# A streaming encoder layer on one core: the input projection by seven products for eight, with token normalisation and rotary tables moved to the first stage

## The reference

```python
h = rmsnorm(x, g_mix)
proj = h @ w_in + b_in                       # 1024 x 2304
qa = rotary(proj[..., :512]);  ka = rotary(proj[..., 512:640]);  va = proj[..., 640:768]
qb, kb, vb = proj[..., 768:1280], proj[..., 1280:1792], proj[..., 1792:]
oa = window_sink_gqa(qa, ka, va, sinks)      # 8 query heads, 2 key heads, window of 128
ob = chunk_relbias_attention(qb, kb, vb, rel_bias)   # 8 heads, own and 8 chunks before
x = x + concat(rmsnorm(oa), rmsnorm(ob)) @ w_out
x = x + memory_cross_attention(rmsnorm(x), rmsnorm(mem), ...)
h = rmsnorm(x, g_ffn)
x = x + (silu(h @ w_gate) * (h @ w_up)) @ w_down
return rmsnorm(x, g_final)

def rotary(t, positions):                    # heads of 64, halves of 32
    ang = positions[..., None] * inv_freq
    t1, t2 = t[..., :32], t[..., 32:]
    return concat([t1 * cos(ang) - t2 * sin(ang), t2 * cos(ang) + t1 * sin(ang)])
```

## Time and profile before

| | us |
|---|---|
| median of 3 runs | 2964.43 (2963.25 to 2970.74) |
| the profiled execution | 2965.04 |
| its span, first to last instruction | 2963.2 |
| PE busy | 2784.1 (94%) |
| DVE busy | 1598.7 (54%) |
| POOL busy | 1052.1 (36%) |
| ACT busy | 1063.8 (36%) |

### The profile page before, as it was taken

The page is one execution under the profiler, slowest core; times in us unless marked ns, Lnnn a source line. Parts: engine busy times, 40 slices in busy tenths (PEclk is TensorE's granted clock), DMA queues, the critical chain, the costliest instruction groups (busy, mean ns, idle before and its releaser), DMA issues. The chain is left out here.

```text
span 2963.2 us, 39417 instructions
## 1 busy us (share of the span) xinstructions
PE 2784.1 (94%) x14112; PEld 2353.4 (79%) x14112; DVE 1598.7 (54%) x2913; ACT 1063.8 (36%) x2101; POOL 1052.1 (36%) x756
## 2 busy tenths in 40 slices
PE   7898989979999899799998799999999998999998
PEld 7786868769999788688887588888788887788876
DVE  3247446457779533233333566666766665654354
ACT  5333333246666422233332333333333332222242
POOL 6644344311100011311222555555555553453152
PEclk9899999979999999899999899999999999999999
DMA  7655666476575433312223433335433333744454
GB/s 237 221 186 197 225 217 215 151 178 158 142 165 136 150 128 128 127 61 75 86 75 114 163 105 97 97 105 170 143 107 96 104 107 113 274 141 145 147 169 131
DMA packets 244535, 428.47 MB, mean 145 GB/s; under 512 B 17792, under 2 KB 151424, under 8 KB 239104
## 3 DMA queue, kind: packets, MB, share of 16 engines
q1 hardware_dynamic: 222416, 406.15, 43.0%
q10 hardware_dynamic: 21936, 19.93, 2.4%
HBM read 285.50 MB, written 135.27 MB: 142 GB/s over the span
## 5 line engine op out<-in xcount | busy, mean ns | idle before, releaser
L50 PE MATMUL gu_acc<-gu_t,shared_m 128*128 128x512 f32 x880 | 344.4, 391 | 10.0 <-DVE gu_t L2348 6.5
L51 PE MATMUL gu_acc<-gu_t,shared_m 128*128 128x512 f32 x880 | 343.9, 391 | 0.0
L52 PE MATMUL gu_acc<-gu_t,shared_m 128*128 128x512 f32 x880 | 343.7, 391 | 0.0
L334 POOL TENSOR_TENSOR front_wq_lo<-front_wq_raw,front_wq_hi 128x1024 fp32r<-128x1024 f32 x72 | 179.1, 2489 | 234.0 <-ACT front_wq_hi L330 233.4
L1424 PE MATMUL att_sum_o<-att_v,att_turned_sb 128*128 128x64 f32 x1616 | 203.0, 270 | 0.0
L50 PEld LDWEIGHTS gu_acc<-gu_t,shared_m 128*128 128x128 f32 x880 | 166.1, 189 | 46.2 <-issue 6.9
L1424 PEld LDWEIGHTS att_sum_o<-att_v,att_turned_sb 128*128 128x128 f32 x1616 | 197.2, 193 | 0.2
L52 PEld LDWEIGHTS gu_acc<-gu_t,shared_m 128*128 128x128 f32 x880 | 166.2, 189 | 34.6
L51 PEld LDWEIGHTS gu_acc<-gu_t,shared_m 128*128 128x128 f32 x880 | 166.1, 189 | 34.6
L1394 PE MATMUL att_sum_s<-att_k,att_q 128*128 128x320 f32 (+3 forms) x704 | 146.1, 327 | 25.4 <-DMA att_k<-qk_d 25.1
L330 ACT ACTIVATE front_wq_hi<-front_wq_raw 128x1024 fp32r<-128x1024 f32 x72 | 76.3, 1059 | 251.1 <-PE qkv_acc L52 149.1
(11 more groups left out here) (310 smaller groups left out, 7310.8 us busy)
## 6 DMA issues: line engine op xcount, KB each, us to landing
front_wq_raw<-in_w_in SPq DMA_DIRECT2D x72, 512.0 KB, 5.2
down_a<-a_d SPq DMA_DIRECT2D x37, 704.0 KB, 4.1
ahead_w_even<-in_w_gate SPq DMA_DIRECT2D x44, 512.0 KB, 4.4
more_w_odd<-in_w_up SPq DMA_DIRECT2D x44, 512.0 KB, 4.3
a_d<-gu_a_mix SPq DMA_DIRECT2D x88, 256.0 KB, 3.1
att_k<-qk_d SPq DMA_DIRECT2D x36, 512.0 KB, 13.2
a_d<-gu_a SPq DMA_DIRECT2D x66, 256.0 KB, 4.2
shared_m<-a_d SPq DMA_DIRECT2D x19, 704.0 KB, 4.3
```

The lines of the kernel that those rows point to most:

```text
L50: pe.matmul(out, l_hi, r_hi, start=first, stop=False)
L51: pe.matmul(out, l_hi, r_lo, start=False, stop=False)
L52: return pe.matmul(out, l_lo, r_hi, start=False, stop=last)
L334: pool.tensor_tensor(self.lo[:, i % Q_SLOTS, :], self.raw[:, i % Q_SLOTS, :], raw(self.hi[:, i % Q_SLOTS, :]), ALU.subtract).then_inc(self ...
```

## The change

The projection is done in two halves of 1024 tokens. In a half, features are taken as 9 pairs of tiles, and tokens as two blocks of 512; with the contraction cut in two this is a 2 x 2 by 2 x 2 product of blocks, done in 7 products of 12 matmuls (4 over half the contraction, three each). POOL makes the combined weights, DVE the four results from the seven products. The order of the pairs is `PAIRS_IN`: `u` is kept as it is, `v` values, `r` rotated queries, and `x` holds rotated keys and the other values.

The token operands of the seven products are made in `stage_products`, which normalises and transposes all 16 token tiles; ACT copies each transposed tile whole (`whole`), DVE makes four combinations of each pair of tiles (`mix_pair`), and SP stores all seven operands to `t_d`. `stage_qkv` loads them, ACT rounds and DVE subtracts. The operand of product 0 and the first weights are loaded at the end of `stage_products` (`ahead`, a class that gate-and-up uses too, with two operands). The sines and cosines of all tokens are also made in `stage_products`, stored to `trig_d` and loaded by half.

The rotated tiles hold first halves of four heads in one tile and second halves in the other, row by row, so that no swap is needed: POOL multiplies by the sine, DVE by the cosine and adds. Attention reads them back with a stride over the rows (`qk_d` has 14 tiles instead of 13). The table of relative positions is made for one head at a time instead of four.

```diff
-        SQUARE, SCALE, TURN = (2, 6, 24, 40), (3, 7, 28, 41), (5, 14, 34, 43)
-        RSQRT, LOAD = (6, 10, 15, 19), (5, 5, 11, 15)
+        TURN = [stage_at(j, 0) for j in range(NT)]
+        SCALE = [stage_at(j, -3) for j in range(NT)]
+        SQUARE = [stage_at(j, -7) for j in range(NT)]
+        WHOLE = [stage_at(j, 2) for j in range(NT)]
+        MIX = [stage_at(2 * i + 1, 5) for i in range(HT)]
+        PUT = [stage_at(j, 6) for j in range(NT)]
+        PUT_MIX = [stage_at(2 * i + 1, 12) for i in range(HT)]
+        TABLE = [[at_share((16 + 22 * b + 5 * part) / 106) for part in range(4)] for b in range(N_BLK)]
...
+                sp.wait_ge(s_plain[0], 16 * 3 * UNITS // 2)
+                sp.wait_ge(s_plain[1], 16 * 3 * UNITS // 2)
+                sp.wait_ge(s_mst, 16 * 4 * UNITS)
+                ahead.load(sp)
+                store(GROUPS - 1)
...
+                def mix_pair(i):
+                    dve.wait_ge(rows.s_lo, 2 * MT + 4 * i + 4)
+                    if i >= 1:
+                        dve.wait_ge(s_mst, 64 * i)
+                    first, second = h[:, 2 * i % 4, :, :], h[:, (2 * i + 1) % 4, :, :]
+                    h11, h21, h12, h22 = first[:, 0:KH, :], first[:, KH:KT, :], second[:, 0:KH, :], second[:, KH:KT, :]
+                    t1, t2, t3, t4 = (mixed[:, m, :, :] for m in range(4))
+                    dve.tensor_tensor(t1, h12, h11, ALU.subtract).then_inc(s_mixed, 1)
+                    dve.wait_ge(s_mixed, 4 * i + 1)
+                    dve.tensor_tensor(t2, h22, t1, ALU.subtract).then_inc(s_mixed, 1)
+                    dve.tensor_tensor(t3, h22, h12, ALU.subtract).then_inc(s_mixed, 1)
+                    dve.wait_ge(s_mixed, 4 * i + 2)
+                    dve.tensor_tensor(t4, t2, h21, ALU.subtract).then_inc(s_mixed, 1)
...
+        PAIRS = len(PAIRS_IN)
+        KP = HALVES * PAIRS
+        TOTAL = KP * N_PROD
+        RESULT = {1: 0, 4: 1, 5: 2, 6: 3}
+        TILE, TOKENS = (0, 1, 1, 0), (0, 0, 1, 1)
+        ROTATE = {0: (0, 1), 1: (3, 2)}
...
+        def split_due(s):
+            kp, q = split_at(s)
+            due = []
+            before, g = result_at(s - 1)
+            if before is not None and kind(before) == "u":
+                due.append((before, g))
+            if q == 0 and rotated(kp - 1):
+                due += [(kp - 1, g) for g in ROTATE[0]]
+            if q == 3 and rotated(kp - 1):
+                due += [(kp - 1, g) for g in ROTATE[1]]
+            return due
...
+                for q in range(first.count, N_PROD):
+                    load_t(0, q)
+                    if q == 2:
+                        load(1)
...
+                    r = rot_index(kp, z)
+                    pool.wait_ge(s_trig, 32 * (kp // PAIRS) + 32)
+                    for g in ROTATE[z]:
+                        summed(pool, kp, g)
+                    if r >= 1:
+                        pool.wait_ge(s_rot, 2 * r)
+                    for i, g in enumerate(reversed(ROTATE[z])):
+                        pool.tensor_tensor(turned_part[:, i, :], y[:, g, :], trig[:, 1, z, :], ALU.mult
+                                           ).then_inc(s_part, 1)
...
+                for kp in range(KP + 2):
+                    if kp < KP:
+                        sums(kp)
+                    sin_products(kp - 2, 1)
+                    if 0 < kp < KP:
+                        low(kp * N_PROD)
+                        low(kp * N_PROD + 1)
+                    sin_products(kp - 1, 0)
...
-                def rotate(r):
-                    dve.wait_ge(s_swap[r % 2], 64 * (r // 2) + 64)
-                    dve.tensor_tensor(swapped[:, r % 2, :], swapped[:, r % 2, :], sin[:, r // Q_ROT % 2, :],
-                                      ALU.mult).then_inc(s_part, 1)
-                    dve.wait_ge(s_part, part_count(r))
-                    dve.tensor_tensor(y[:, r % 3, :], cos_part[:, r % 2, :], swapped[:, r % 2, :],
-                                      ALU.add).then_inc(s_sum, 1)
+                def rotate(kp, z):
+                    r = rot_index(kp, z)
+                    a, b = ROTATE[z]
+                    if values(kp):
+                        dve.wait_ge(s_vt, max(value_place[kp, g] for g in (a, b)) + 1)
+                    dve.wait_ge(s_part, 2 * r + 2)
+                    for g in (a, b):
+                        dve.tensor_tensor(y[:, g, :], y[:, g, :], trig[:, 0, z, :], ALU.mult).then_inc(s_cos, 1)
+                    dve.wait_ge(s_cos, 2 * r + 1)
+                    dve.tensor_tensor(y[:, a, :], y[:, a, :], turned_part[:, 0, :], ALU.subtract).then_inc(s_rot, 1)
+                    dve.wait_ge(s_cos, 2 * r + 2)
+                    dve.tensor_tensor(y[:, b, :], y[:, b, :], turned_part[:, 1, :], ALU.add).then_inc(s_rot, 1)
...
+                for q in range(first.count, N_PROD):
+                    t_low(0, q)
+                    if q in SUMS and q < RS:
+                        w_low(q)
+                dve.wait_ge(s_const, 16)
+                for s in range(END):
+                    kp, q = split_at(s)
+                    if RS <= s + RS - 1 < TOTAL and split_at(s + RS - 1)[1] in SUMS:
+                        w_low(s + RS - 1)
+                    if TURN0 + 3 <= s < TURN0 + 3 + N_PROD:
+                        t_low(1, s - TURN0 - 3)
+                    if q == 6 and rotated(kp):
+                        rotate(kp, 0)
+                    if q == 2 and rotated(kp - 1):
+                        rotate(kp - 1, 1)
+                    for what in split_due(s - 1):
+                        if rotated(what[0]):
+                            low(*what)
+                    for what in split_due(s):
+                        if not rotated(what[0]):
+                            low(*what)
+                    if s < TOTAL:
+                        combine(s)
...
-                    for k in range(KT):
-                        wk = slice(k * P, (k + 1) * P)
-                        last = split3(pe, acc[i % ACCS][:, :], weights.hi[:, i % Q_SLOTS, wk],
-                                      weights.lo[:, i % Q_SLOTS, wk], hs[b % 2][0][:, k, :], hs[b % 2][1][:, k, :],
-                                      k == 0, k == KT - 1)
-                    last.then_inc(weights.s_acc, 1)
+                    for k in range(KH):
+                        if fresh and k % 2 == 0:
+                            pe.wait_ge(s_tlo, 2 * (kp // PAIRS * N_PROD + q) + k // 2 + 1)
+                        wk, tk = slice(k * P, (k + 1) * P), slice(k * BANK, (k + 1) * BANK)
+                        last = split3(pe, acc[s % ACCS][:, :], w_hi[s % RS][:, wk], w_lo[s % RS][:, wk],
+                                      t_hi[q][:, tk], t_lo[q][:, tk], k == 0, k == KH - 1)
+                    last.then_inc(s_prod, 1)
+                    before = result_at(s - 1)
+                    if before in value_place:
+                        turn(value_place[before])
```

1254 lines of the change are left out of this document (686 added, 568 removed).

## The result

The changed kernel takes 3029.1 us (median of 4 runs, 3027.4 to 3031.8) against 2967.0 us for the kernel before in the same session (4 runs, 2963.3 to 2970.7): a ratio of 1.021 with a 95% interval of 1.0193 to 1.0228. It is slower by some 62 us, where 2950 us was forecast with a range of 2910 to 2982.

What follows compares the result with a forecast made beforehand. PE, busy 94% of the span, was taken as the bound, with DVE and POOL taking turns in the first stage. First stage +50.5, projection -59.1, gap before attention -5.6 us gave 2950 us, range 2910 to 2982.

Steps and rivals of the forecast that it cites:

- The projection's slots: Projection: 126 products of 2.72 us make 342.7 us of PE slots, plus 10.8 us for 24 groups of value transposes.
- Start: Projection's start: PE stops after product 2 until result 0, behind all six operand subtractions on DVE; 20 us lost.
- Middle: Projection's second half: operands loaded over the first's cost 8.8 us as in gate-and-up, plus 3 for value transposes; 12 us.
- Rotated pairs: Projection: DVE lags some 7 us, covered except in the value pair after the last rotated one; 3.5 us each half.
- The slower rival: Projection: DVE's lag passes the five products' lead (13.6 us), rotated pairs cost 54 us instead of 7; 2998 us, chance 0.12.
- The gap before attention: Between projection and attention: the last pair is not rotated, leaving some 2.2 us of work instead of 7.8; -5.6 us.
- The first stage's work: First stage: DVE and POOL work on SBUF mostly passes one after the other, taking 150 us from 15.85 us on.
- The tail: First stage's end: last combination stored, then product 0's operand loaded, rounded and subtracted before the next matmul; 19 us.
- port hidden: First stage: DVE and POOL mostly work at different moments, PE's 104.5 us rule; stage ends at 139, time 2905, chance 0.15.
- Full exclusion: First stage: DVE and POOL exclude each other wholly, 164.6 us instead of 150; time 2966, no change, chance 0.20.

Runs made afterwards that it cites:

- e2: Changed kernel with pair order u0, v0, x, u1, r0, u2, r1, v1, u3, so no value pair comes first in a half; 3023.6 us.
- e1: Changed kernel with pair order v0, u0, v1, x, u1, r0, u2, r1, u3, so v1 no longer follows r1; 3012.8 us.
- e16: Joined kernel with short rotary tables, pairs reordered to u0, v0, v1, x, r0, u1, r1, u2, u3; 2981.2 us.
- e15: Changed kernel with the low parts of the first stage's weights made on DVE instead of POOL; 3012.5 us.
- e5: Changed kernel with stores of the mixed operands issued two steps after they are made instead of seven; 3011.7 us.
- e8: Changed kernel without DVE's four combining subtractions per pair of row tiles, as many bytes stored from the turned rows; 3014.2 us.
- e4: Changed kernel without 15 of the 17 rotary table instructions per block on DVE in the first stage; 3014.2 us.
- e9: Changed kernel with four buffers for x instead of two and the mixed operands' stores issued early; 3009.3 us.
- e10: Changed kernel with four buffers for the rows of x in the first stage instead of two, nothing else; 3021.9 us.
- e14: Joined kernel (early mixed stores, four x buffers, earlier first-block loads, reordered pairs) with 10 table instructions per block on DVE instead of 17; 2968.5 us.
- e3: Changed kernel with the projection's first-block loads issued once half 0's stores have landed, not after half 1's last store; 3017.5 us.
- e6: Changed kernel with operands stored in 2 KB pieces instead of 512 bytes and read by the matmuls with a stride; 3025.9 us.
- e12: Joined kernel (early mixed stores, four x buffers, earlier first-block loads, reordered pairs) with operands stored in 2 KB pieces; 2973.2 us.
- e11: Changed kernel with early mixed stores, four x buffers, earlier first-block loads and pair order u0, v0, v1, x, u1, r0, u2, r1, u3; 2973.4 us.

## Why the prediction was wrong, step by step

- **The projection's slots (342.7 + 10.8):** right. 1608 instructions, and 0.221 to 0.227 us each wherever PE is not held.
- **Start (20 us):** 20.1 measured, with result 0 on DVE 26.3 us after the first matmul, where 27 was reckoned. The size is right and the reason half right: in e2 the order without transposes still loses 16, so the transposes add 4; the rest is the operands' arrival.
- **Middle (12 us):** 16.1, 4 us more than gate-and-up's price and the 3 us added to it.
- **Rotated pairs (7 us): the first step that failed.** "DVE then lags some 7 us. Operands are prepared five products ahead (13.6 us), which covers it", and 3.5 us in the value pair. The lag was right: v1's first result starts on DVE 7.2 and 6.6 us after PE has finished its product. What failed is the 3.5 us for it, which counts one stop. It cost 17.0 and 15.9: PE stops for the first result (5.3 and 4.7 us) and again for the second (3.9 and 4.8), because r1's second rotation, which the forecast had seen waiting for POOL, stands on DVE between the two; other waits and the lower clock make the rest. e1 shows it by its end: with v1 out of that place the loss there is gone. The slower rival, "the rotated pairs set the pace", asked for a lag above 13.6 us; between x and v1 it is 11.8 at most, at u2's last result, and in e1 three rotated pairs run at nearly full pace with plain pairs between. Only e16, without a plain pair between x and r0, comes near it (13.9 us, at the last result of the pair behind r0).
- **The gap before attention (-5.6):** -4.
- **The first stage's work (150 us from 15.85 on): the step that failed most.** It was 185.75. "I therefore count what must pass one after the other": I added up the work of two engines that get in each other's way, and took for granted that DVE never stands idle and that loads and stores keep up. The lengthening was even overpriced: in DVE's order 155 to 160 us, of which 96.7 its own work, so some 60 for POOL's remainders; DVE was busy 132.6, 44 more than the 88.5 (126.8 less 38.3) that its own work takes in e15. What was put at nothing is DVE's idle time, 53 us. The runs name parts of it: `mixed`, one buffer stored seven steps late (13 us: e5, e8; e4 and e15 gain as much by other ways), two buffers for x (5 to 10: e9, e10), and table work in DVE's order (6: e14). With all of these the stage ends at 176.9, still 11 us above the forecast's 165.85, and the cause of that stays open. The diff had both numbers, the one `mixed` buffer and the offset of 12, and I priced the 56 stores at nothing without naming what would hide them.
- **The tail (19 us):** 22.3, the mechanism as forecast; e3 shows that 10 of it were avoidable.
- **The rival "port hidden" (139 us)** is excluded by every run. **"Full exclusion" (164.6)** gave the better number, but by luck: e15 has next to no exclusion and takes 172.

With the losses that the runs could remove, the terms come back near the forecast's: e14's projection starts at 187.8 (forecast 185), but takes 402.7 (392.5), and its gap is 19 (14.3), so 53.4 - 48.9 - 0.9 = +3.6 us where -14 was forecast. Even well placed, this change moves as much into the first stage as it takes from the projection.

## What to carry to other kernels

A sum of engine work is a floor, not a forecast: for each buffer that new work goes through, write down when it is filled, when its store is issued and when it is needed again, and see whether that loop is longer than the interval of the tiles. Where several edits each give the same gain and stop at the same time, don't add their gains: they probably act on one loop, and the next bound is already there; only joined runs price them. And where an in-order engine lags behind the one that sets the pace, look for the next results that are read without slack: the lag is paid there, here twice within one pair, so put those results ahead of the work that makes the lag.

## What was not expected of the hardware

- One DVE subtraction of 512 columns (L650) took 2461 ns on average beside POOL's instead of 692, longer than the 1771 of the earlier trace rows. POOL's have 1024 columns here and take 2.6 us each; two of L650's seven start at 69.73 and 94.72 us while POOL is in one, and end 0.55 us after POOL's.
- Taking POOL's 30 subtractions over to DVE (38 us more work) left DVE busy 6 us less (126.8 against 132.6): here DVE did both engines' subtractions in less busy time than its own beside POOL's.
- Stops cost twice. In e1 the projection is 18.5 us shorter, but PE is idle in it only 9.3 us less (44.2 against 53.5); for the same 1608 instructions it is busy 9.1 us less (364.5 against 373.6). They run slower around stops: the mean granted clock was 0.77 in 443 to 473 us of the changed kernel, 0.91 and 0.89 around v1, and 1.00 in 473 to 573.
- The strided read of operands in 128-column pieces (e6) did not slow the matmuls: from 473 to 573 us PE gets 455 instructions, 452 in the changed kernel, and the projection takes 428.1 us, 427.2 there. In e12 the same edit has the projection at 406.3 where e11 has 401.3; 20 instructions of that are missing in the middle (154 in 390.3 to 450.3 us, 174 in e11's 391.9 to 451.9), and why is open.
